# Per-head mean squares of the second block's queries and keys: column sums and turns replaced by a block-diagonal product with full-width roots

## The chip, the cores and the metric

The kernel runs on one core of a Trainium2 chip. The metric is the device time of one execution in microseconds (us), the median of several runs. Everything that follows comes from those times and from one execution recorded by the hardware profiler.

## What is computed

The program is two transformer blocks over 512 tokens of width 1024, all in float32. The change touches one step of the second block, the normalisation of its attention queries and keys:

```python
def rms_norm(x, g):
    xf = x.astype(jnp.float32)
    y = xf * lax.rsqrt(jnp.mean(xf * xf, axis=-1, keepdims=True) + RMS_EPS)
    return (y * g.astype(jnp.float32)).astype(x.dtype)

# in token_mixer of the second block
xin = h @ w_in
qa, ka, va, qm, km, vm, og, ig, fg = jnp.split(xin, cuts, axis=-1)
qa = rms_norm(qa.reshape(B, S, N_ATTN_HEADS, ATTN_HEAD_DIM), q_norm_g) * ATTN_SCALE
ka = rms_norm(ka.reshape(B, S, N_ATTN_HEADS, ATTN_HEAD_DIM), k_norm_g)
```

There are 8 heads of 64 columns, 512 tokens. So queries and keys are each 512 x 512, and each 64-long piece of a column is divided by the root of its own mean square.

## The kernel before, in words

**Layout.** Activations lie with features on the 128 partitions and the 512 tokens along the row, so a query tile `q[:, r, :]` is 128 features (two heads) by 512 tokens. Queries are four such tiles (r = 0 to 3), keys four more (r = 4 to 7). One head's mean square is a sum over 64 partitions.

**Products.** Weights come in blocks of 1 MB (`w_raw`, two buffers). ScalarE copies a block to its high part (`w_hi`, L1147), GpSimd takes the difference as the low part (`w_lo`, L489), and TensorE makes each float32 product out of three fp32r ones: high by high, high by low and low by high. An output tile of 128 x 512 is 24 matmuls (L569 to L571, or L586 to L588 for a pair, L618 to L620 for the value tiles). Everything on TensorE stands in one hand-written order; each engine runs its own list in order and they meet by semaphores.

**The order around the change.** TensorE's loop over the blocks j of the second block's input product (L995 on) has two slots per block, t = 2j and 2j + 1; each slot is one tile (t = 0 and 1, and t = 2 and 3, are pairs). Slots 0 to 3 make the queries, 4 to 7 the keys, 8 to 11 the values, slot 12 the narrow gate columns (slot 13 is empty), slots 14 on the queries and keys of the mLSTM. After slot 12 come the first attention scores (L649), which wait for all eight normalised tiles (`qk_normed` at 8).

ScalarE has the same loop (from L1508): after a tile it copies it out of its bank (L1534), squares it into one of two buffers `g[:, r % 2]` (L1535), and frees the bank. Before that it waits for the sums of the tile two before (`qn_ss`). In odd slots it also splits a weight block (L1147). VectorE's loop (from L2262) starts only behind eight products that scale `x` by the final gain (L2232, L2233).

**The norms before.** `qk_sums(r)` (L951, its matmuls L958): for each of the four groups of 128 tokens, the squares stand as the stationary operand and two columns of 1 and 0 move past them, which gives a 128 x 2 piece of sums with tokens on partitions, in bank 6. It stands after slot 3 (r = 0 and 1), slot 4 (2 and 3) and slots 5 to 8 (4 to 7). `qk_columns(e)` (L2236 on): for four tiles at once VectorE takes the mean (L2239), ScalarE the root of 128 x 32 values (L1539), VectorE inverts and refines it once (reciprocal L1732 and four small operations), and spreads it to four tiles of 128 x 512 (L2244). `qk_turn(r)` (L962, transposes L968) turns these back to features on partitions, two tiles each after slots 5, 6, 9 and 10. `qk_norm(r)` (L2251) is one VectorE operation per tile.

```python
for r in {3: (0, 1), 4: (2, 3)}.get(t + u, (t + u - 1,) if 5 <= t + u <= 8 else ()):
    qk_sums(r)
```

Of the kernel before, what the change touches and what calls it, by code (L numbers as in the profile page):

```python
# [13 lines left out]
P = 128  # L14
# [133 lines left out]
def two_blocks(nc, weights, ada, c_rows, consts, rope, tri_bias, mult_bias, tri_mask, layer_params, params, x_in, selectors, out):  # L148
    with ExitStack() as ctx:
# [49 lines left out]
        b_hi = sb("b_hi", [P, KT, S], F32R, two)  # L199
        b_lo = sb("b_lo", [P, KT, S], F32R, two)  # L200
        two.close()
        one.enter_context(nc.sbuf_tensor("region_1", [P, 2 * KT * S], F32))
        ctx.enter_context(one)

# [30 lines left out]
        next_gain = sb("next_gain", [P, KT])  # L235
        shift_parts = sb("shift_parts", [P, KT, 2], F32R)
        shift_sum = sb("shift_sum", [P, 2])

        ps = [ctx.enter_context(nc.psum_tensor(f"ps{b}", [P, S], F32)) for b in range(8)]

# [79 lines left out]
        gate_split = sem("gate_split")  # L320
        gate_scaled = sem("gate_scaled")
        qn_sq = sem("qn_sq")
        qn_ss = sem("qn_ss")
        qn_ms = sem("qn_ms")
        qn_root = sem("qn_root")
        qn_spread = sem("qn_spread")
        qn_turned = sem("qn_turned")
        qk_normed = sem("qk_normed")
        v2_ready = sem("v2_ready")
        mc_first = sem("mc_first")  # L330
# [219 lines left out]
        def _(pe):  # L550
# [397 lines left out]
                            last.then_inc(tile_done, 1)  # L948
                shift_rows(s, 1)

            def qk_sums(r):  # L951

                pe.wait_ge(qn_sq, r + 1)
                if r == AT:
                    pe.wait_ge(qn_ms, 1)
                c = 8 * (r % AT)
                for tt in range(TT):
                    last = nc.tensor.matmul(ps[6][:, c + 2 * tt:c + 2 * tt + 2], g[:, r % 2, tt * P:(tt + 1) * P],  # L958
                                            half[:, 0:P:HD], start=True, stop=True)
                last.then_inc(qn_ss, 1)  # L960

            def qk_turn(r):  # L962

                pe.wait_ge(qn_spread, r + 1)
                if r >= 2:
                    pe.wait_ge(qk_normed, r - 1)
                for tt in range(TT):
                    last = nc.tensor.transpose(ps[4 + r % 2][:, tt * P:(tt + 1) * P],  # L968
                                               g[:, 2 + r % AT, tt * P:(tt + 1) * P], ident)
                last.then_inc(qn_turned, 1)  # L970

            def a_turns():

# [21 lines left out]
            for j in range(C_OUT):  # L995
                s, t = j % 2, 2 * j
                low = low_parts(L, 4 * j)
                if j == 0:
                    plain_pair(s, low)
                    continue  # L1000
                if j == 1:
                    for u in range(2):
                        pe.wait_ge(bank_free[t + u], nth(L, LAYER_BANKS, BANK_USES[t + u]))
                    tile_pair([ps[t + u][:, :] for u in range(2)], s, (a_hi, a_lo), normed_ready(0), low)
                for u in range(2):
                    if C_VA <= j < C_IF or C_VM <= j < C_OG:
                        first = C_VA if j < C_IF else C_VM
                        token_tiles(L, 2 * first, s, (2 * u, 2 * u + 1), j - first, low, lambda n: BANK_USES[n])
                    elif j == C_IF:
                        if u == 0:  # L1010
                            tile(L, t, s, KT, 0, a_hi, a_lo, low, m=F_ROW + MH, tiles=2)
                    elif j > 1:
                        tile(L, t + u, s, KT, u * P, a_hi, a_lo, low)
                    for r in {3: (0, 1), 4: (2, 3)}.get(t + u, (t + u - 1,) if 5 <= t + u <= 8 else ()):
                        qk_sums(r)
                    for first in (AT + 1, 2 * AT + 1):
                        if t + u - first in (0, 1):
                            for e in range(2):
                                qk_turn(first - AT - 1 + 2 * (t + u - first) + e)
# [123 lines left out]
        def _(act):  # L1143
# [328 lines left out]


            L = LAYERS
            nc.scalar.activation(warm[:, :], ones[:, 0:1], ACT.Sqrt)
            nc.scalar.activation(shift_parts[:, :, 0], mod[:, 0:KT], ACT.Copy).then_inc(shift_hi, 1)
            act.wait_ge(ms_ready, nth(L, 2, 0))
# [22 lines left out]
            def silu_tanh(i):  # L1500

                act.wait_ge(mc_ready, i + 1)
                if i > 0:
                    act.wait_ge(mc_silu, i)
                nc.scalar.activation(mt[:, :], g[:, 4 + i % 2, :], ACT.Tanh, scale=0.5
                                     ).then_inc(mc_tanh, 1)

            for j in range(C_OUT):  # L1508
                for u in range(2):
                    t = 2 * j + u  # L1510
# [4 lines left out]
                    elif j in (C_VA, C_VM):  # L1515
                        if u:
                            act.wait_ge(v_halves, nth(L, 1, (C_VA, C_VM).index(j)))
                    else:
                        act.wait_ge(tile_done, nth(L, LAYER_TILES, t))
                    if j == 0:  # L1520
                        act.wait_ge(plain_scaled, t + 1)
                        nc.scalar.activation(g[:, t, :], g[:, 6 + t, :], ACT.Square, bias=shift_sum[:, t:t + 1]
                                             ).then_inc(qn_sq, 1)
                    if u and j > 0:
                        w_split(L, j + 2)
# [2 lines left out]
                            nc.scalar.activation(q[:, i, :], g[:, 6 + i, :], ACT.Identity, bias=shift_sum[:, i:i + 1])  # L1528
                        act.drain()
                    if 0 < j < C_VA:  # L1530
                        act.wait_ge(qn_ss, t - 1)
                        dst = q[:, t, :] if t < AT else k[:, t - AT, :]
                        if t >= 2:
                            nc.scalar.activation(dst, ps[b][:, :], ACT.Copy)  # L1534
                            nc.scalar.activation(g[:, t % 2, :], ps[b][:, :], ACT.Square).then_inc(qn_sq, 1)  # L1535
                            act.drain().then_inc(bank_free[b], 1)
                    if t in (AT, 2 * AT):
                        act.wait_ge(qn_ms, t // AT)
                        nc.scalar.activation(qcol[:, 1, :], qcol[:, 0, :], ACT.Sqrt).then_inc(qn_root, 1)  # L1539
# [170 lines left out]
        def _(dve):  # L1710
# [90 lines left out]
            nc.vector.memset(top[:, 1, 2:3], 0.0).then_inc(s1_split, 1)  # L1801
            nc.vector.memset(top[:, 1, 3:4], 0.0).then_inc(p1_used, 1)
            nc.vector.memset(mod[:, :], 0.0)
            dve.wait_ge(params_loaded, 16)
            for n in range(KT):
                dve.wait_ge(x_loaded[n // 2] if n > 0 else x_first, 16)
# [429 lines left out]
            def qk_columns(e):  # L2236

                dve.wait_ge(qn_ss, AT * (e + 1))
                nc.vector.tensor_scalar(qcol[:, 0, :], ps[6][:, 0:32], 1.0 / HD, EPS, ALU.mult, ALU.add).then_inc(qn_ms, 1)  # L2239
                dve.wait_ge(qn_root, e + 1)  # L2240
                refine(qcol[:, 2, :], qcol[:, 1, :], qcol[:, 0, :], qcol[:, 1, :])
                dve.drain()
                for r in range(AT):
                    nc.vector.tensor_copy(g[:, 2 + r, :].rearrange("p (t c) -> p t c", t=2 * TT),  # L2244
                                          qcol[:, 2, 8 * r:8 * r + 8].unsqueeze(2).to_broadcast([P, 2 * TT, HD])
                                          ).then_inc(qn_spread, 1)

            def qk_norm(r):
                dst, gain = (q[:, r, :], SP_QG) if r < AT else (k[:, r - AT, :], SP_KG)
                dve.wait_ge(qn_turned, r + 1)  # L2250
                nc.vector.scalar_tensor_tensor(dst, dst, sp[:, gain:gain + 1], ps[4 + r % 2][:, :], ALU.mult, ALU.mult  # L2251
                                               ).then_inc(qk_normed, 1)

            def m_gaps(h):
# [7 lines left out]
            for j in range(C_OUT):  # L2262
                for u in range(2):
                    t = 2 * j + u
                    b = t % 4
                    if t in (AT, 2 * AT):
                        qk_columns(t // AT - 1)
                    for first in (AT + 1, 2 * AT + 1):
                        if t - first in (0, 1):
                            for e in range(2):  # L2270
                                qk_norm(first - AT - 1 + 2 * (t - first) + e)
                            dve.drain()
# [272 lines left out]
def constant_matrices():  # L2545
# [4 lines left out]
            m[base + half + i, K_ROT + base + i] = -1.0  # L2550
            m[base + i, K_ROT + base + half + i] = 1.0
    for base in (0, HD):
        m[base:base + HD, K_HALF + base:K_HALF + base + HD] = 1.0
    m[:, K_ID:K_ID + P] = np.eye(P, dtype=np.float32)
    m[:, K_ONES:K_ONES + P] = 1.0
    return m
# [106 lines left out]
```

## Time and profile before

| | us |
|---|---|
| median of 3 runs | 2041.26 |
| lowest and highest run | 2041.17, 2041.50 |
| the profiled execution, first to last instruction (its span) | 2039.8 |
| TensorE busy in it | 2032.7 |
| VectorE, ScalarE, GpSimd busy | 1217.6, 897.0, 1041.2 |
| mean granted TensorE clock | 0.999 of full speed |

The time around the profiled execution's instructions has no row of its own; the span is what the profile gives, and the median of the runs is 1.5 us above it. The first row of the page says which engine is busy, the chain that ended last says on whom the end waits. Starts are microseconds from the first instruction. Matmuls overlap, so the cost of one is read from the distance between two starts, not from its own duration.

### The profile page before, as it was taken

The page shows a single profiled execution, that of the slowest core. Times are in us where ns is not written, and L with a number is a line of the kernel's source. Part 1 is how long each engine was busy: PE and PEld are TensorE (multiplying, and loading weights), DVE is VectorE, ACT ScalarE, POOL GpSimd, SP SyncE. Part 2 cuts the span into 40 slices and gives each one's busy share as a digit, 9 for nine tenths or more (in the row PEclk, how much of TensorE's full clock was granted, in tenths as well). Part 3 has the DMA queues.
Part 4 walks back from the last instruction along what each step waited for, and adds up shares of the span by engine and source line. Part 5 has one row for each costly group of instructions (what it writes and reads, how often), then busy time and mean ns, then how long its engine had stood idle before and what let it go on. Part 6 is the DMA issues. An engine that isn't in the chain of part 4 may idle for free.

```text
span 2039.8 us, 29841 instructions
## 1 busy us (share of the span) xinstructions
PE 2032.7 (100%) x10920; PEld 1715.4 (84%) x10920; DVE 1217.6 (60%) x2154; ACT 897.0 (44%) x1367; POOL 1041.2 (51%) x773
## 2 busy tenths in 40 slices
PE   9999999999999999999999999999999999999999
PEld 7788778889889877877788899898877788989898
DVE  4677336476757637854365767567445478747363
ACT  4124353536446422144445355364446544535352
POOL 5454335476565754544355755556343324556555
PEclk9999999999999999999999999999999999999999
DMA  6322212343543232221223344422221212223223
GB/s 216 99 95 93 83 62 97 121 159 111 186 145 125 104 117 95 94 96 62 83 103 133 135 157 145 165 104 104 80 102 62 83 42 95 92 104 104 104 104 104
DMA packets 36084, 222.61 MB, mean 109 GB/s; under 512 B 5308, under 2 KB 5692, under 8 KB 10336
## 3 DMA queue, kind: packets, MB, share of 16 engines
q1 hardware_dynamic: 28608, 190.66, 26.7%
q10 hardware_dynamic: 7328, 30.00, 4.3%
q8 instruction: 91, 1.49, 0.3%
q14 instruction: 57, 0.47, 0.1%
HBM read 215.65 MB, written 2.10 MB: 107 GB/s over the span
## 4 chain that ended last, share of the span: by engine, by line
PE 98%; DVE 1%; DVEq 0%; ACT 0%; DMA 0%; issue 0%; ACTq 0%
PE ps L569 18%; PE ps L571 18%; PE ps L570 18%; PE ps L733 6%; PE ps L735 6%; PE ps L734 6%; PE ps L586 4%; PE ps L587 4%; PE ps L588 4%; PE ps L649 2%; PE ps L618 1%; PE ps L620 1%; PE ps L619 1%; PE ps L670 1%; PE ps L659 1%; PE ps L703 0%
## 5 line engine op out<-in xcount | busy, mean ns | idle before, releaser
L489 POOL TENSOR_TENSOR w_lo<-w_raw,w_hi 128x512 fp32r<-128x512 f32 x544 | 734.2, 1380 | 780.8 <-ACT w_hi L1147 771.1
L1147 ACT ACTIVATE w_hi<-w_raw 128x2048 fp32r<-128x2048 f32 x134 | 256.1, 1911 | 387.8 <-PE ps L571 288.0
L569 PE MATMUL ps<-a_hi,w_hi 128*128 128x512 f32 (+1 forms) x888 | 351.8, 396 | 0.0
L571 PE MATMUL ps<-a_hi,w_lo 128*128 128x512 f32 (+1 forms) x888 | 346.2, 390 | 0.0
L570 PE MATMUL ps<-a_lo,w_hi 128*128 128x512 f32 (+1 forms) x888 | 345.8, 389 | 0.0
L503 POOL TENSOR_TENSOR w_lo<-w_raw,w_hi 128x512 fp32r<-128x512 f32 x164 | 214.7, 1331 | 160.2 <-ACT w_hi L1281 160.2
L569 PE MATMUL ps<-b_hi,w_hi 128*128 128x512 f32 x612 | 238.1, 389 | 0.0
L570 PE MATMUL ps<-b_lo,w_hi 128*128 128x512 f32 x612 | 238.1, 389 | 0.0
L571 PE MATMUL ps<-b_hi,w_lo 128*128 128x512 f32 x612 | 238.1, 389 | 0.0
L569 PEld LDWEIGHTS ps<-a_hi,w_hi 128*128 128x128 f32 (+1 forms) x888 | 165.3, 186 | 47.3 <-issue 10.8
L571 PEld LDWEIGHTS ps<-a_hi,w_lo 128*128 128x128 f32 (+1 forms) x888 | 165.3, 186 | 37.1
L570 PEld LDWEIGHTS ps<-a_lo,w_hi 128*128 128x128 f32 (+1 forms) x888 | 165.4, 186 | 34.4
L571 PEld LDWEIGHTS ps<-b_hi,w_lo 128*128 128x128 f32 x612 | 114.9, 188 | 24.0
L569 PEld LDWEIGHTS ps<-b_hi,w_hi 128*128 128x128 f32 x612 | 114.9, 188 | 23.8
L570 PEld LDWEIGHTS ps<-b_lo,w_hi 128*128 128x128 f32 x612 | 114.9, 188 | 23.7
L733 PE MATMUL ps<-a_hi,w_hi 128*128 128x256 f32 x424 | 120.2, 284 | 0.6 <-ACTq L1693 0.3
L734 PE MATMUL ps<-a_lo,w_hi 128*128 128x256 f32 x424 | 120.0, 283 | 0.0
L735 PE MATMUL ps<-a_hi,w_lo 128*128 128x256 f32 x424 | 120.0, 283 | 0.0
L1281 ACT ACTIVATE w_hi<-w_raw 128x1024 fp32r<-128x1024 f32 x82 | 85.7, 1052 | 61.1 <-DVE w_raw L1712 27.1
L1712 DVE TENSOR_TENSOR g<-ps,g 128x512 f32<-128x512 f32 (+1 forms) x116 | 73.5, 633 | 42.2 <-ACT g L1424 16.6
L1712 DVE TENSOR_TENSOR b_lo<-g,b_hi 128x512 fp32r<-128x512 f32 x86 | 63.0, 735 | 47.6 <-ACT b_hi L1410 36.2
L1825 DVE CUSTOM_DVE_ANT_0 pr<-ps,bias 128x512 f32<-128x512 f32 (+3 forms) x48 | 21.5, 486 | 114.9 <-issue 114.9
(394 smaller groups left out, 4535.0 us busy)
## 6 DMA issues: line engine op xcount, KB each, us to landing
w_raw<-in_weights SPq DMA_DIRECT2D x176, 1024.0 KB, 4.9
v<-in_ada ACTq DMA_DIRECT2D x24, 1024.0 KB, 4.9
out<-x SPq DMA_DIRECT2D x8, 256.0 KB, 2.2
x<-in_x_in SPq DMA_DIRECT2D x3, 512.0 KB, 7.0
w_raw<-in_weights SPq DMA_DIRECT2D x4, 256.0 KB, 5.7
yc<-in_c_rows ACTq DMA_DIRECT2D x2, 512.0 KB, 3.1
bias<-in_mult_bias ACTq DMA_DIRECT2D x1, 640.0 KB
x<-in_x_in SPq DMA_DIRECT2D x2, 256.0 KB, 4.9
```

Of the source, the lines that this page charges most:

```text
L489: nc.gpsimd.tensor_tensor(w_lo[:, s, piece], w_raw[:, s, piece], f32(w_hi[:, s, piece]), ALU.subtract).then_inc(w_lo_ready, 1)
L503: nc.gpsimd.tensor_tensor(quad(w_lo, s, u, kh), quad(w_raw, s, u, kh), f32(quad(w_hi, s, u, kh)), ALU.subtract).then_inc(w_lo_ready, 1)
L569: nc.tensor.matmul(o, wh, hi(kt), start=kt == 0, stop=False)
L570: nc.tensor.matmul(o, wh, lo(kt), start=False, stop=False)
L571: last = nc.tensor.matmul(o, wl, hi(kt), start=False, stop=kt == depth - 1)
L586: nc.tensor.matmul(o[u], wh, src[0][:, kt, :], start=kt == 0, stop=False)
L733: nc.tensor.matmul(o, fh[:, kt, :], mh[:, kt, :], start=kt == 0, stop=False)
L734: nc.tensor.matmul(o, fh[:, kt, :], ml[:, kt, :], start=False, stop=False)
L735: last = nc.tensor.matmul(o, fl[:, kt, :], mh[:, kt, :], start=False, stop=kt == HK - 1)
L1147: nc.scalar.activation(w_hi[:, n % 2, :], w_raw[:, n % 2, :], ACT.Copy).then_inc(w_hi_ready, 1)
L1281: return nc.scalar.activation(hi, raw, ACT.Copy)
L1712: return nc.vector.tensor_tensor(out_, a, b_, op)
```

## The change

It replaces the column sums, the narrow roots and the turns by an operation of full width for each tile.

- A 128 x 128 matrix `heads_mean` holds 1/64 in two diagonal blocks of 64 (the constant itself is changed from 1 to 1/64). ScalarE makes an fp32r copy of it once.
- ScalarE squares each tile twice: to float32 (`g[:, r % 2]`) and to fp32r (`sq_parts[..., 0, ...]`). VectorE subtracts them (`qk_low`), which gives the low part.
- TensorE (`qk_means`) makes two matmuls of 128 x 512, high and low part, into bank 4 or 5, one call after each of slots 3 to 10. From r = 2 on it waits for the norm of the tile two before.
- ScalarE (`qk_root`) takes the root of 128 x 512 means out of the bank, at the head of slots 4 to 11.
- VectorE (`qk_norm`) inverts 128 x 512 values, refines with three further operations, and multiplies.

Five semaphores go or are renamed; `qk_sums`, `qk_turn` and `qk_columns` go.

```diff
+        sq_parts = sb("sq_parts", [P, 2, 2, S], F32R, eleven)
+        heads_mean = sb("heads_mean", [P, P], F32R)
+        eps = sb("eps", [P, 1])
...
-            def qk_sums(r):
-                pe.wait_ge(qn_sq, r + 1)
-                if r == AT:
-                    pe.wait_ge(qn_ms, 1)
-                c = 8 * (r % AT)
-                for tt in range(TT):
-                    last = nc.tensor.matmul(ps[6][:, c + 2 * tt:c + 2 * tt + 2], g[:, r % 2, tt * P:(tt + 1) * P],
-                                            half[:, 0:P:HD], start=True, stop=True)
-                last.then_inc(qn_ss, 1)
-            def qk_turn(r):
-                pe.wait_ge(qn_spread, r + 1)
+            def qk_means(r):
+                pe.wait_ge(qn_split, r + 1)
                 if r >= 2:
                     pe.wait_ge(qk_normed, r - 1)
-                for tt in range(TT):
-                    last = nc.tensor.transpose(ps[4 + r % 2][:, tt * P:(tt + 1) * P],
-                                               g[:, 2 + r % AT, tt * P:(tt + 1) * P], ident)
-                last.then_inc(qn_turned, 1)
+                for e in range(2):
+                    last = nc.tensor.matmul(ps[4 + r % 2][:, :], heads_mean[:, :], sq_parts[:, r % 2, e, :],
+                                            start=e == 0, stop=e == 1)
+                last.then_inc(qn_ss, 1)
...
+                    if 3 <= t + u < 3 + 2 * AT:
+                        qk_means(t + u - 3)
...
+            nc.scalar.activation(heads_mean[:, :], half, ACT.Copy)
...
+            def qk_root(r):
+                act.wait_ge(qn_ss, r + 1)
+                if r >= 2:
+                    act.wait_ge(qk_normed, r - 1)
+                nc.scalar.activation(g[:, 2 + r % 2, :], ps[4 + r % 2][:, :], ACT.Sqrt, bias=eps[:, :]).then_inc(qn_root, 1)
...
+                    if 4 <= t < 4 + 2 * AT:
+                        qk_root(t - 4)
                     if j == 0:
                         act.wait_ge(plain_scaled, t + 1)
-                        nc.scalar.activation(g[:, t, :], g[:, 6 + t, :], ACT.Square, bias=shift_sum[:, t:t + 1]
+                        nc.scalar.activation(g[:, t, :], g[:, 6 + t, :], ACT.Square, bias=shift_sum[:, t:t + 1])
+                        nc.scalar.activation(sq_parts[:, t, 0, :], g[:, 6 + t, :], ACT.Square, bias=shift_sum[:, t:t + 1]
                                              ).then_inc(qn_sq, 1)
...
                     if 0 < j < C_VA:
-                        act.wait_ge(qn_ss, t - 1)
                         dst = q[:, t, :] if t < AT else k[:, t - AT, :]
                         if t >= 2:
                             nc.scalar.activation(dst, ps[b][:, :], ACT.Copy)
-                            nc.scalar.activation(g[:, t % 2, :], ps[b][:, :], ACT.Square).then_inc(qn_sq, 1)
+                            act.wait_ge(qn_ss, t - 1)
+                            nc.scalar.activation(g[:, t % 2, :], ps[b][:, :], ACT.Square)
+                            nc.scalar.activation(sq_parts[:, t % 2, 0, :], ps[b][:, :], ACT.Square).then_inc(qn_sq, 1)
                             act.drain().then_inc(bank_free[b], 1)
-                    if t in (AT, 2 * AT):
-                        act.wait_ge(qn_ms, t // AT)
-                        nc.scalar.activation(qcol[:, 1, :], qcol[:, 0, :], ACT.Sqrt).then_inc(qn_root, 1)
...
+            def qk_low(r):
+                dve.wait_ge(qn_sq, r + 1)
+                tt(sq_parts[:, r % 2, 1, :], g[:, r % 2, :], f32(sq_parts[:, r % 2, 0, :]), ALU.subtract
+                   ).then_inc(qn_split, 1)
+            def qk_norm(r):
+                dst, gain = (q[:, r, :], SP_QG) if r < AT else (k[:, r - AT, :], SP_KG)
+                mean_, root_, y = ps[4 + r % 2][:, :], g[:, 2 + r % 2, :], g[:, 4 + r % 2, :]
+                dve.wait_ge(qn_root, r + 1)
+                nc.vector.reciprocal(y, root_)
                 dve.drain()
+                nc.vector.scalar_tensor_tensor(root_, mean_, EPS, y, ALU.add, ALU.mult)
+                dve.drain()
+                nc.vector.scalar_tensor_tensor(root_, root_, -0.5, y, ALU.mult, ALU.mult)
+                dve.drain()
+                nc.vector.scalar_tensor_tensor(root_, root_, 1.5, y, ALU.add, ALU.mult)
+                dve.drain()
+                nc.vector.scalar_tensor_tensor(dst, dst, sp[:, gain:gain + 1], root_, ALU.mult, ALU.mult
                                                ).then_inc(qk_normed, 1)
...
-                    if t in (AT, 2 * AT):
-                        qk_columns(t // AT - 1)
-                    for first in (AT + 1, 2 * AT + 1):
-                        if t - first in (0, 1):
-                            for e in range(2):
-                                qk_norm(first - AT - 1 + 2 * (t - first) + e)
-                            dve.drain()
+                    if 4 <= t < 4 + 2 * AT:
+                        qk_norm(t - 4)
+                    if t < 2 * AT:
+                        qk_low(t)
...
-        m[base:base + HD, K_HALF + base:K_HALF + base + HD] = 1.0
+        m[base:base + HD, K_HALF + base:K_HALF + base + HD] = 1.0 / HD
```

## Rows read from the trace of the kernel before

**Rows 1.** The page: span, busy time of engines, and chain that ended last.
```profile
span 2039.8 us, 29841 instructions
PE 2032.7 (100%) x10920; PEld 1715.4 (84%) x10920; DVE 1217.6 (60%) x2154; ACT 897.0 (44%) x1367; POOL 1041.2 (51%) x773
...
PE 98%; DVE 1%; DVEq 0%; ACT 0%; DMA 0%; issue 0%; ACTq 0%
```

**Rows 2.** Timeline of PE, slots 3 to 12 (start, length, instruction, count).
```profile
1441.25 1.84 PE L958 MATMUL ps<-kc,g 128*128 128x2 f32 x16
1442.95 0.49 PE L569 MATMUL ps<-a_hi,w_hi 128*128 128x512 f32 x1
...
1448.53 1.84 PE L958 MATMUL ps<-kc,g 128*128 128x2 f32 x16
...
1455.82 0.95 PE L958 MATMUL ps<-kc,g 128*128 128x2 f32 x8
1456.63 1.07 PE L968 MATMUL ps<-kc,g 128*128 128x128 f32 x8
1457.46 0.47 PE L569 MATMUL ps<-a_hi,w_hi 128*128 128x512 f32 x1
...
1459.61 0.39 PE L569 MATMUL ps<-a_hi,w_hi 128*128 128x512 f32 x1
...
1463.01 0.95 PE L958 MATMUL ps<-kc,g 128*128 128x2 f32 x8
...
1501.18 1.13 PE L649 MATMUL ps<-k,q 64*128 64x512 f32 x4
```

**Rows 3.** Timeline of DVE, 1428 to 1500 us.
```profile
1440.49 5.34 DVE L2233 SCALAR_TENSOR_TENSOR x<-x,sp,ps 128x512 f32<-128x512 f32 x8
```

**Rows 4.** Timeline of ACT, 1428 to 1500 us.
```profile
1442.29 0.60 ACT L1534 ACTIVATE q<-ps 128x512 f32<-128x512 f32 x1 [0.84 <-PE ps L958]
1442.79 0.59 ACT L1535 ACTIVATE g<-ps 128x512 f32<-128x512 f32 x1
1443.55 1.92 ACT L1147 ACTIVATE w_hi<-w_raw 128x2048 fp32r<-128x2048 f32 x1 [0.17 <-issue]
```

**Rows 5.** Groups of DVE by form: reciprocals and a small product, 1405 to 1530 us.
```profile
L1732 DVE RECIPROCAL qcol<-qcol 128x32 f32<-128x32 f32 x2 | 0.7, 354 | 0.7 <-ACT qcol L1539 0.7
L1721 DVE RECIPROCAL ps<-qcol 128x8 f32<-128x8 f32 x1 | 0.2, 198 | 0.0
L1723 DVE SCALAR_TENSOR_TENSOR qcol<-ps,qcol 128x8 f32<-128x8 f32 x1 | 0.2, 167 | 0.1
```

**Rows 6.** Groups of DVE by form, operations 512 wide; a timeline of three with drains between.
```profile
L2390 DVE SCALAR_TENSOR_TENSOR pt<-ps,pr 128x512 f32<-128x512 f32 x2 | 1.4, 692 | 4.0 <-PE ps L1041 4.0
L2320 DVE SCALAR_TENSOR_TENSOR yc<-mt,g 128x512 f32<-128x512 f32 x3 | 2.1, 703 | 1.6 <-ACT mt L1505 1.5
L2213 DVE SCALAR_TENSOR_TENSOR a_lo<-g,mod,a_hi 128x512 fp32r<-128x512 f32 x8 | 6.0, 747 | 0.3
...
1514.20 2.40 DVE L2309 SCALAR_TENSOR_TENSOR g<-ps,sp,g 128x511 f32<-128x511 f32 x3
```

**Rows 7.** Timeline of DVE and POOL, 1395 to 1403 us: one operation beside GpSimd and alone.
```profile
1395.21 2.54 POOL L489 TENSOR_TENSOR w_lo<-w_raw,w_hi 128x512 fp32r<-128x512 f32 x2
1397.09 1.22 DVE L1777 SCALAR_TENSOR_TENSOR a_lo<-x,next_gain,a_hi 128x512 fp32r<-128x512 f32 x1 [0.21 <-issue]
...
1402.53 0.75 DVE L1777 SCALAR_TENSOR_TENSOR a_lo<-x,next_gain,a_hi 128x512 fp32r<-128x512 f32 x1 [0.22 <-issue]
```

**Rows 8.** Windows at the block's entry: busy of PE, PEld, DVE, ACT, POOL; granted clock.
```profile
1416.00:1417.00 1.00, 0.57 (x5) 0.58 (x6) 1.00 (x2) 1.00 (x1) 0.00 (x0) 1.00 0.00 0
...
1418.00:1419.00 1.00, 1.00 (x5) 1.00 (x5) 0.22 (x2) 0.75 (x3) 1.00 (x2) 0.50 0.00 0
...
1420.00:1421.00 1.00, 1.00 (x4) 0.81 (x3) 0.78 (x4) 0.00 (x0) 1.00 (x2) 0.50 0.02 8
```

**Rows 9.** Who waited for whom on PE: the one of its six groups that lies at this block's entry (total, times, longest).
```profile
PE ps L861 <- DVE yc L1790: 0.7, 1, 0.7
```

More of the change, by code:

```diff
@@ L201, in two_blocks @@
         two.close()
+        eleven = ExitStack()
+        sb("front_11", [P, (2 * AT + 3) * S], F32, eleven)
+        sq_parts = sb("sq_parts", [P, 2, 2, S], F32R, eleven)
+        eleven.close()
         one.enter_context(nc.sbuf_tensor("region_1", [P, 2 * KT * S], F32))
@@ L322, in two_blocks @@
         qn_sq = sem("qn_sq")
+        qn_split = sem("qn_split")
         qn_ss = sem("qn_ss")
-        qn_ms = sem("qn_ms")
         qn_root = sem("qn_root")
-        qn_spread = sem("qn_spread")
-        qn_turned = sem("qn_turned")
         qk_normed = sem("qk_normed")
@@ L1013, in _ @@
                         tile(L, t + u, s, KT, u * P, a_hi, a_lo, low)
-                    for r in {3: (0, 1), 4: (2, 3)}.get(t + u, (t + u - 1,) if 5 <= t + u <= 8 else ()):
-                        qk_sums(r)
-                    for first in (AT + 1, 2 * AT + 1):
-                        if t + u - first in (0, 1):
-                            for e in range(2):
-                                qk_turn(first - AT - 1 + 2 * (t + u - first) + e)
+                    if 3 <= t + u < 3 + 2 * AT:
+                        qk_means(t + u - 3)
                     pair, part = divmod(HEAD2_SLOTS.index(t + u), 4) if t + u in HEAD2_SLOTS else (-1, 0)
@@ L1803, in _ @@
             nc.vector.memset(mod[:, :], 0.0)
+            nc.vector.memset(eps[:, :], EPS)
             dve.wait_ge(params_loaded, 16)
@@ L2234, in _ @@
                                                ALU.mult, ALU.mult)
[L2236 to L2241, printed above, removed]
-                dve.drain()
[L2243 to L2246, printed above, removed]
+            def qk_low(r):
+                dve.wait_ge(qn_sq, r + 1)
+                tt(sq_parts[:, r % 2, 1, :], g[:, r % 2, :], f32(sq_parts[:, r % 2, 0, :]), ALU.subtract
+                   ).then_inc(qn_split, 1)
             def qk_norm(r):
                 dst, gain = (q[:, r, :], SP_QG) if r < AT else (k[:, r - AT, :], SP_KG)
-                dve.wait_ge(qn_turned, r + 1)
-                nc.vector.scalar_tensor_tensor(dst, dst, sp[:, gain:gain + 1], ps[4 + r % 2][:, :], ALU.mult, ALU.mult
+                mean_, root_, y = ps[4 + r % 2][:, :], g[:, 2 + r % 2, :], g[:, 4 + r % 2, :]
[7 more added lines that the diff above has]
+                nc.vector.scalar_tensor_tensor(root_, root_, 1.5, y, ALU.add, ALU.mult)
+                dve.drain()
+                nc.vector.scalar_tensor_tensor(dst, dst, sp[:, gain:gain + 1], root_, ALU.mult, ALU.mult
                                                ).then_inc(qk_normed, 1)
@@ L2265, in _ @@
                     b = t % 4
-                    if t in (AT, 2 * AT):
-                        qk_columns(t // AT - 1)
-                    for first in (AT + 1, 2 * AT + 1):
-                        if t - first in (0, 1):
-                            for e in range(2):
-                                qk_norm(first - AT - 1 + 2 * (t - first) + e)
-                            dve.drain()
+                    if 4 <= t < 4 + 2 * AT:
+                        qk_norm(t - 4)
+                    if t < 2 * AT:
+                        qk_low(t)
                     if j == C_IF:
```

## The prediction

> **What bounds the kernel now.** The page first: TensorE is busy for 2032.7 of 2039.8 us and makes 98% of the chain that ended last [rows 1]. In the waits of TensorE the longest in this part of the program is 0.7 us [rows 9]. So the end moves by what TensorE gains or loses, one for one, and the other engines are hidden as long as nothing on TensorE waits for them. The change adds waits, so the second thing to read is how far ahead of TensorE those engines are. For that I read its timeline from slot 3 to slot 12, then VectorE's and ScalarE's beside it.
>
> **TensorE's own work.** Two calls of the column sums take 1441.25 to 1442.95, 1.70 us, and again 1.70 after slot 4; a single call after slot 5 takes 1455.82 to 1456.63, 0.81, and there are four of those; two turns take 1456.63 to 1457.46, 0.83, and there are four such pairs [rows 2]. Sum: 2 x 1.70 + 4 x 0.81 + 4 x 0.83 = 9.96 us. Fifteen product matmuls take 1459.61 to 1463.01, 0.227 each, so a tile of 24 is 5.44; slot 4 takes 1442.95 to 1448.53, 5.58 [rows 2]. The 0.14 is the change-over after the float32 work; eight times 1.0 us (estimate, from that one tile). Removed: 11.0 us. Added: 16 fp32r matmuls of the width of a product, 16 x 0.227 = 3.6. Alone this would make the kernel 7.4 us faster. One 128 x 128 copy on ScalarE at the block's entry and one memset at the start are small and beside a busy TensorE: nothing.
>
> **The first wait.** The first mean product stands right behind slot 3, at 1441.25, and now needs VectorE's low part. VectorE's eight gain products run 1440.49 to 1445.83 [rows 3], and the low part stands behind them. In the old order VectorE had no part in the sums, so this cost nothing. The low part has both operands in SBUF, 0.70 us by the like row [rows 6], done 1446.5. I add 0.3 for the signal and the weight load ahead of the matmul (estimate; ScalarE's 0.17 between a drain and its next instruction is the nearest [rows 4]): TensorE resumes at 1446.8, 5.5 us late.
>
> Such a gap also costs clock. At the block's entry, after 0.7 us of waiting [rows 9] and a window in which TensorE was busy 0.57 with narrow float32 products, the granted clock stood at 0.50, the 1.2 GHz level, from 1418 to 1421 us [rows 8]. Three microseconds at half speed lose about 1.6. A gap of 5.5 is longer, so I take 1.6 once, with bounds of 0 (the drop falls inside the gap) and 3.
>
> **The chain per tile.** From r = 2 on TensorE's means of tile r wait for the norm of r - 2; ScalarE's squares of r + 2 wait for these means; the root of r - 1 stands behind these squares on ScalarE; and the norm of r - 1 waits for that root. That is a loop once per tile, whose length is set by no tile product. Its terms:
> - VectorE's norm. Four 512-wide operations: 0.69 with a PSUM operand, 0.70 and 0.70 with both in SBUF, 0.75 with a column scalar too [rows 6]. A drain adds 0.08: three operations of 0.75 take 2.40 from first start to last end with two drains between [rows 6]. With four drains: 0.69 + 0.70 + 0.70 + 0.75 + 0.32 = 3.16.
> - The reciprocal at 128 x 512 is in no row. At 8 elements it takes 198 ns, at 32 it takes 354 [rows 5]: 6.5 ns per further element, so 354 + 480 x 6.5 = 3.47 us. From below: a product of 8 takes 167 ns beside 198 [rows 5], and were a wide reciprocal no dearer than a wide product, it would take 0.7. From above, the whole 354 ns taken as proportional gives 354 x 16 = 5.7. I take 3.47, since the slope is from the same operation.
> - After the norm: signal and weight load 0.3, two mean matmuls to the end of the second 0.23 + 0.39 = 0.62, signal 0.1, two squares of 0.59 spaced by 0.50 (as L1534 and L1535 are) 1.09, drain and issue 0.17 [rows 4]. The wide root is like the 0.59 of a copy out of a bank and I give it 0.70 for the bias column. Signal 0.07. Together 3.05.
>
> One turn of the loop: 3.16 + 3.47 + 3.05 = 9.7 us. TensorE has 5.44 + 0.45 = 5.9 us of work in it, and waits 3.8. (The low part of r + 2, 0.70, fits beside the root.)
>
> By the Trainium skill (VectorE: DVE Perf Modes, Walkthrough: the 8-slice pipeline in each mode, First, the fixed hardware budget) a reciprocal is an iterative divide with a repeat count of 8; at the 0.96 GHz it gives, my estimate is 4.27 us for 512 elements and a sum 6 us higher. The two rows above give 6.5 ns per element rather than 8.3, and the sum stays with them.
>
> **VectorE beside GpSimd.** The same operation with both inputs in SBUF takes 1.22 us while GpSimd splits weights and 0.75 alone [rows 7]. In slots 5, 7 and 11 ScalarE's weight split follows directly on the root, GpSimd then works about 5 us, and the last three operations of norms 1, 3 and 7 lie under it: 3 x 0.47 = 1.4 each. For norm 4, which meets the split of slot 9 at its end, I take 0.5.
>
> **The sum, in time.**
> - Means 0 from 1446.8 to 1447.3; slot 4 with the slow clock ends 1447.3 + 5.44 + 1.6 = 1454.3.
> - Means 1 end 1454.9, squares 3 end 1456.1, root 0 ends 1457.0, norm 0 runs 1457.1 to 1463.7.
> - Norms 1 to 4, one turn of the loop each: + 4 x 9.7 + 1.4 + 1.4 + 0.5 = 1505.8.
> - No squares follow tile 7, so norms 5 and 6 run back to back: + 2 x 6.7 = 1519.2. TensorE has its last two wait-bound calls here (means 6 and 7); slot 11 ends about 1518.5.
> - Root 7 waits for slot 11 and ends 1519.4; norm 7 ends 1519.4 + 0.1 + 6.6 + 1.4 = 1527.5.
> - The scores wait for all eight norms: 1527.8 with signal and weight load. Slot 12 ends at 1524.0, so this is a wait too. In the old trace they start at 1501.18 [rows 2].
>
> Difference + 26.6. Behind the scores the order is the old one, and TensorE is again the bound. The ledger agrees: - 7.4 of work, + 5.5 + 1.6 for the first gap, about + 23 for five waits of 3.8 to 5.2 and one of 1.3 after slots 5 to 10, + 3.8 before the scores. The profiled execution would have a span of 2066.4; against the median of the runs, 1.5 us above the span of before, I forecast 2041.26 + 26.6 = **2067.9 us**.
>
> **Rivals.**
> 1. *The loop fits under the tiles, and the narrow work goes for nothing (faster).* Then only the TensorE ledger counts: 2041.26 - 7.4 = 2033.9, with the first wait gone as well. It needs a loop of at most 5.9 us. The 3.05 around the norm and the 3.16 of its four products alone are 6.2, so it decides against it even with a free reciprocal; only shorter signals or operations than in any row would bring it. Chance 0.03.
> 2. *Only the first wait binds.* The reciprocal is as cheap as a product and all else is slightly shorter: - 7.4 + 5.5 + 0 to 1.6 gives 2039.4 to 2041.0. For it speaks that the reciprocal's width is extrapolated over a factor of 16; against it the slope. Chance 0.03.
> 3. *The loop binds, but with a reciprocal well under the slope.* At 2.5 us each of the eight norms is 1.0 shorter, less what the tiles of slots 9 to 11 then set: 2061. Chance 0.1.
> 4. *A longer norm.* Were the slope beyond 32 elements a quarter steeper than between 8 and 32 (354 + 480 x 8.1 = 4.25 us), or GpSimd in the reciprocal's way too, each norm would be 0.8 longer, eight times: 2067.9 + 6.4 = 2074. For it speaks that two short operations, mostly fixed cost, carry the slope. Chance 0.16. The Trainium skill's rule above gives about this time.
> 5. *The clock falls again and again.* Each wait of 3.8 us could bring the 1.2 GHz level as in [rows 8]. In the middle that is mostly hidden, since a slow tile of at most 7.5 us still fits in 9.7; the mean matmuls in the loop would cost 0.4 more a turn, and the last wait up to 1.6 after the scores: 2067.9 + 7 x 0.4 + 1.6 = 2072.3. Chance 0.18.
>
> The forecast itself has 0.5. A measurement can tell about 0.2% (4 us) from no change. **Faster** by more than that: 0.03. **Within** it: 0.03, rival 2 and all its edges. **Slower**: 0.94. The range takes in rivals 3, 4 and 5 with the bounds of the clock and of the contention (none at all is - 5): 2057 to 2077.
>
> **What the changed profile would show.** Among the waits of TensorE a new line for the mean products, released by VectorE: one of 5 to 6 us and five or six of 3 to 4.5. A reciprocal of 128 x 512, eight of them, at 3.4 to 3.5 us: the term on which most hangs, 8 us of the sum per 1 us. Mean products about 9.7 us apart from the third on. Scores starting near 1528. A window at 0.50 clock in slot 4. I am wrong if TensorE shows no waits there, or if the eight reciprocals take under 1 us.

## The result and the profile after

| | before | after |
|---|---|---|
| median of the runs shown with the result (5 each), us | 2041.26 | 2071.80 |
| ratio, with its 95% interval | | 1.015 [1.0140, 1.0161] |
| span of the profiled execution, us | 2039.8 | 2071.4 |
| mean granted TensorE clock | 0.999 | 0.992 |

The kernel is 1.5% slower, 30.5 us; 26.6 were forecast (2067.9, with a range of 2057 to 2077). Where did the time go? The page of the changed kernel, to be read against [rows 1]:

```profile
span 2071.4 us, 29735 instructions
PE 2039.0 (98%) x10840; PEld 1715.5 (83%) x10840; DVE 1269.2 (61%) x2175; ACT 906.1 (44%) x1382; POOL 1042.5 (50%) x773
...
PE 93%; DVE 4%; DVEq 1%; ACT 1%; issue 0%; DMA 0%; ACTq 0%; POOL 0%
```

TensorE's share of the chain that ended last falls from 98 to 93%, and VectorE has 4 in place of 1. VectorE's busy time grows by 51.6 us. That it is 61% busy over the whole program tells nothing here: 50.4 of the 51.6 us lie in a stretch of 91 (1440 to 1531, where the same work before took 61). The profiled execution is the slowest of the five (2073.21 us). TensorE is idle 32.4 us (span less busy) where it was idle 7.1, and its own busy time is not less but 6.3 more, although it has 80 instructions fewer. Both need a closer look. First, for whom it waits (total, times, longest), which answers to [rows 9]:

```profile
PE ps L961 <- DVE q L2254: 13.2, 4, 5.0
PE ps L961 <- DVE sq_parts L1710: 5.1, 1, 5.1
PE ps L653 <- DVE k L2254: 3.6, 1, 3.6
PE ps L961 <- DVE k L2254: 3.5, 2, 1.8
```

L961 are the mean products, L2254 the last operation of a norm, L653 the first scores. The sum is 25.4 us: one wait for the first low part (5.1), four and two for norms of the two tiles before (13.2 and 3.5), one before the scores (3.6). The mean products in TensorE's timeline, and the scores, which answer to the last of [rows 2]:

```profile
1446.44 1.22 PE L961 MATMUL ps<-sq_parts,heads_mean 128*128 128x512 f32 x2 [5.08 <-DVE sq_parts L1710]
1453.90 0.62 PE L961 MATMUL ps<-sq_parts,heads_mean 128*128 128x512 f32 x2
1463.20 1.19 PE L961 MATMUL ps<-sq_parts,heads_mean 128*128 128x512 f32 x2 [3.20 <-DVE q L2254]
1474.82 1.19 PE L961 MATMUL ps<-sq_parts,heads_mean 128*128 128x512 f32 x2 [3.86 <-DVE q L2254]
1484.68 0.71 PE L961 MATMUL ps<-sq_parts,heads_mean 128*128 128x512 f32 x2 [1.17 <-DVE q L2254]
1495.82 1.19 PE L961 MATMUL ps<-sq_parts,heads_mean 128*128 128x512 f32 x2 [4.95 <-DVE q L2254]
1505.94 0.71 PE L961 MATMUL ps<-sq_parts,heads_mean 128*128 128x512 f32 x2 [1.66 <-DVE k L2254]
1513.91 0.78 PE L961 MATMUL ps<-sq_parts,heads_mean 128*128 128x512 f32 x2 [1.81 <-DVE k L2254]
...
1530.79 1.44 PE L653 MATMUL ps<-k,q 64*128 64x512 f32 x4 [3.64 <-DVE k L2254]
```

From 1463.20 to 1505.94 they stand 11.6, 9.9, 11.1 and 10.1 us apart, where a tile with its mean product is 5.9 us of work. Where a pair takes 1.19 us and not 0.62, the clock is down. What fills such a turn is in VectorE's timeline, here norm 1 and the beginning of the next turn:

```profile
1465.54 0.69 DVE L1710 TENSOR_TENSOR sq_parts<-g,sq_parts 128x512 fp32r<-128x512 f32 x1 [2.49 <-ACT sq_parts L1536]
1466.39 3.35 DVE L2246 RECIPROCAL g<-g 128x512 f32<-128x512 f32 x1 [0.16 <-ACT g L1503]
1469.82 0.69 DVE L2248 SCALAR_TENSOR_TENSOR g<-ps,g 128x512 f32<-128x512 f32 x1
1470.59 0.75 DVE L2250 SCALAR_TENSOR_TENSOR g<-g 128x512 f32<-128x512 f32 x1
1471.41 1.59 DVE L2252 SCALAR_TENSOR_TENSOR g<-g 128x512 f32<-128x512 f32 x1
1473.09 1.58 DVE L2254 SCALAR_TENSOR_TENSOR q<-q,sp,g 128x512 f32<-128x512 f32 x1
1477.17 0.69 DVE L1710 TENSOR_TENSOR sq_parts<-g,sq_parts 128x512 fp32r<-128x512 f32 x1 [2.49 <-ACT sq_parts L1536]
```

The reciprocal is 3.35 us. The idle 2.49 before each of these low parts is the way through TensorE and ScalarE. The last two operations of norm 1 take 1.6 us where they take 0.69 and 0.75 in norm 0. GpSimd splits weights from 1468.24 to 1474.12. The operation from 1470.59 lies in that stretch too, with both operands in SBUF, and takes 0.75; why it is spared is not shown. And the windows (busy of PE, PEld, DVE, ACT, POOL, then the granted clock), which answer to [rows 8]:

```profile
1442.00:1444.00 2.00, 0.00 (x0) 0.00 (x0) 2.00 (x4) 0.99 (x2) 0.97 (x1) 1.00 0.05 8
...
1446.00:1448.00 2.00, 1.56 (x4) 1.28 (x5) 0.98 (x2) 0.30 (x1) 0.00 (x0) 0.53 0.55 234
1448.00:1450.00 2.00, 2.00 (x7) 1.58 (x6) 0.69 (x1) 1.83 (x3) 0.00 (x0) 0.61 0.00 0
...
1475.00:1480.00 5.00, 5.00 (x12) 3.92 (x13) 2.65 (x2) 2.26 (x4) 0.00 (x0) 0.50 0.60 210
...
1495.00:1500.00 5.00, 4.18 (x10) 3.34 (x11) 2.06 (x3) 1.77 (x3) 0.12 (x1) 0.50 0.63 211
...
1515.00:1520.00 5.00, 5.00 (x18) 3.97 (x17) 4.69 (x5) 0.00 (x0) 0.00 (x0) 0.72 0.34 141
...
1530.00:1535.00 5.00, 4.21 (x11) 2.56 (x12) 3.48 (x8) 1.80 (x2) 0.18 (x1) 0.66 0.61 210
```

TensorE stands at the 1.2 GHz level (0.50), for some microseconds each time, after the first wait, after those of 3.20, 3.86 and 4.95 us, after the last before a mean product (1.81), and after the one before the scores. After the waits of 1.17 and 1.66 us the granted clock is 1.00. This is why its busy time grew: between 1475 and 1480 it was busy throughout and began 12 matmuls, where 22 fit at full clock. How much busy time that is in all, e4 below tells: it has the same 10840 matmuls and no wait in this stretch, and TensorE is busy 2026.5 us in it, 12.5 less than here.

### The profile page after: what moved, and what is told of

It is laid out like the page before. It is cut to its first block, busy times and chain, and to the rows that moved or that the text cites. A ratio compares the mean times of both kernels' runs of the same rounds, so it can differ in the third digit from the quotient of the medians.

```text
span 2071.4 us, 29735 instructions
## 1 busy us (share of the span) xinstructions
PE 2039.0 (98%) x10840; PEld 1715.5 (83%) x10840; DVE 1269.2 (61%) x2175; ACT 906.1 (44%) x1382; POOL 1042.5 (50%) x773
## 4 chain that ended last, share of the span: by engine, by line
PE 93%; DVE 4%; DVEq 1%; ACT 1%; issue 0%; DMA 0%; ACTq 0%; POOL 0%
PE ps L573 18%; PE ps L575 17%; PE ps L574 17%; PE ps L737 6%; PE ps L739 6%; PE ps L738 6%; PE ps L590 3%; PE ps L591 3%; PE ps L592 3%; PE ps L653 2%; PE ps L674 1%; PE ps L663 1%; PE ps L622 1%; PE ps L623 1%; PE ps L624 1%; DVE g L2246 1%
```

## The experiments

All times are medians. The kernel before, run beside them, had 2040.19 us in the first group (e1 to e4), 2041.22 in the second (e7, e10, e9) and 2040.62 in the third (e11, e12). Ratios are to it, with their 95% intervals. The changed kernel stood beside a kernel before of 2041.26 us, so a difference of medians between it and a run of the first group can be 1.1 us too large. The figure in square brackets behind a difference between groups is therefore that of the two distances from the kernel before. Line numbers of an experiment are its own.

### e1_gain_later: the first wait taken away

```diff
                     if t < 2 * AT:
                         qk_low(t)
+                    if t == 1:
+                        for n in range(KT):
+                            final_gain(n)
```
(in place of the same loop ahead of the slots; the means go to `ps[6 + r % 2]`)

> The eight gain products of VectorE move behind the low parts of tiles 0 and 1, and the means go to banks 6 and 7, so that bank 4 stays the gain's. Theory (the first wait and its slow clock shift the whole chain, one for one): no wait of 5 us before the first mean product, norm 0 starts near 1450 instead of 1456.5, and the time falls by 6 to 7 us, to about 2065. Rival (the first wait is absorbed by the later ones, which would grow): the scores start at the same time and the time falls by 1 us or less.

Measured: 2064.11 us, ratio 1.0116 [1.0099, 1.0133], 7.7 us [6.6] below the changed kernel. The row of 5.1 us for the low part is gone from TensorE's waits, and most of the others is left (18.4 us of 20.3):

```profile
PE ps L961 <- DVE q L2254: 12.5, 4, 4.3
PE ps L653 <- DVE k L2254: 3.6, 1, 3.6
PE ps L961 <- DVE k L2254: 2.3, 1, 2.3
```

The scores start at 1521.08, 9.7 us earlier (slot 3 itself ends 1.8 us earlier in this execution, so 7.9 are the change's), and norm 0 begins at 1449.21. So the first wait shifts the chain with all that comes behind it; the later waits do not absorb it.

### e2_copy_for_reciprocal: the norm made shorter

```diff
-                nc.vector.reciprocal(y, root_)
+                nc.vector.tensor_copy(y, root_)
```

> A copy of the same shape stands in place of the reciprocal; the inversion is left out. Theory (the loop's length is the norm's, 3.35 us of it the reciprocal): each norm is 2.9 us shorter, seven or eight of them lie on the chain, and the time falls by 20 to 23 us, to about 2050, with mean products 6.7 us apart in place of 9.6. Rival (the waits come from the handshake between the engines, not from the norm's length): the mean products stay over 8.5 us apart and the time falls by 5 us or less.

Measured: 2050.13 us, ratio 1.0045 [1.0030, 1.0059], 21.7 us [20.6] below the changed kernel. The copy takes 0.43 us. The mean products of tiles 2 to 5 start at 1460.00, 1468.21, 1474.67 and 1482.91, 7.6 us apart on average rather than 6.7, since every second turn has GpSimd in it:

```profile
PE ps L961 <- DVE sq_parts L1710: 5.1, 1, 5.1
PE ps L961 <- DVE q L2254: 4.7, 4, 2.1
PE ps L653 <- DVE k L2254: 0.8, 1, 0.8
```

The waits for norms fall from 20.3 us (13.2 + 3.6 + 3.5) to 5.9 (4.7 + 0.8 and one of 0.4 not shown). The norm's length sets the waits, and the reciprocal is about two thirds of what the change costs.

### e3_four_banks: the handshake loosened

```diff
-                if r >= 2:
-                    pe.wait_ge(qk_normed, r - 1)
+                if r >= 4:
+                    pe.wait_ge(qk_normed, r - 3)
...
-                    last = nc.tensor.matmul(ps[4 + r % 2][:, :], heads_mean[:, :], ...
+                    last = nc.tensor.matmul(ps[4 + r % 4][:, :], heads_mean[:, :], ...
```

> The means take banks 4 to 7 in turn, so TensorE waits for the norm of four tiles before and no more of two before. Theory (with two banks the loop through all engines sets the pace; with four only VectorE's own sum does, about 7.4 us a tile with the low part and GpSimd's share): TensorE waits no more in slots 5 to 9 but some 13 to 15 us before the scores, and the time falls by 12 to 16 us, to about 2058. Rival (VectorE's sum of work was the bound already): the same waits move to the scores and the time stays within 3 us of 2072.

Measured: 2063.23 us, ratio 1.0110 [1.0093, 1.0127], 8.6 us [7.5] below the changed kernel, against 12 to 16 expected. That lies between the theory's 12 to 16 and the rival's 3 at most; the pattern of the waits is the theory's:

```profile
PE ps L653 <- DVE k L2254: 15.2, 1, 15.2
PE ps L961 <- DVE sq_parts L1710: 5.1, 1, 5.1
PE ps L573 <- ACT v L1547: 2.9, 1, 2.9
```

TensorE waits for no norm until the scores and there for 15.2 us. VectorE works from 1455.86 to 1519.66 without a gap that counts: 63.8 us for eight norms and five low parts. One norm there, with both neighbours:

```profile
1493.00 1.08 DVE L2250 SCALAR_TENSOR_TENSOR g<-g 128x512 f32<-128x512 f32 x1
1494.15 1.62 DVE L2252 SCALAR_TENSOR_TENSOR g<-g 128x512 f32<-128x512 f32 x1
1495.86 1.58 DVE L2254 SCALAR_TENSOR_TENSOR k<-k,sp,g 128x512 f32<-128x512 f32 x1
1497.37 3.34 DVE L2246 RECIPROCAL g<-g 128x512 f32<-128x512 f32 x1
```

That is 8.0 us a tile, against 5.9 of TensorE. So loosening the loop through three engines removes the smaller part of the loss; VectorE's sum of work keeps the larger. Three things in the trace go against the expected gain: operations beside GpSimd at 1.6 us (1.2 had been put in), value tiles that ScalarE now frees later, since roots that wait for norms stand ahead of them (2.9 us), and the clock after the long wait, which e10 takes up. How they share it was not separated.

### e4_no_norm_gain_later: TensorE's ledger alone

As e1, with the reciprocal and the three refining lines of `qk_norm` left out.

> As e1_gain_later, and the reciprocal and the three refining products are left out, so that a norm is one product (the output is then multiplied by the root). Theory (TensorE alone is the bound once nothing waits, and its work is 7.4 us less than before): about 2034 us, no wait over 1 us in slots 3 to 12. Rival (the means or the extra ScalarE work cost something of their own): 2037 us or more, or a wait that is left.

Measured: 2034.76 us, ratio 0.9966 [0.9952, 0.9980], that is 6.9 us below before by the ratio and 5.4 by the medians. No wait of TensorE between slots 3 and 12 is left, the mean products stand 5.94 us apart, and the scores start at 1494.30, where before has 1501.18: 6.9 us again, with slot 3 ending at the same time within 0.1 us. The TensorE side of the change is worth about 7 us. Two mean matmuls take 5.94 - 5.44 = 0.50 us there, where the forecast had 0.45.

### e7_four_banks_gain_later

e1 and e3 together (banks 6, 7, 5, 4 in turn), and the roots of tiles 4 to 7 ahead of ScalarE's waits for the value tiles.

> Both mends of waits together: four banks (6, 7, 5, 4 in turn) and the gain products behind the first two low parts; ScalarE also takes roots 4 to 7 ahead of its waits for the value tiles. Theory (with four banks VectorE's list of work sets the end, and it now begins about 6.5 us earlier): about 2057 us, one wait of 14 to 17 us before the scores and no other over 1 us. Rival (with four banks the start does not matter, since TensorE only waits at the end): 2062 us or more.

Measured: 2055.97 us, ratio 1.0069 [1.0054, 1.0085]. One wait of 14.8 us before the scores as expected, 0.5 for the last low part (at 1484.62), and one of 3.6 for a value tile, which the expectation had ruled out. The mends together give 15.8 us [15.8], half of the loss. The other half is VectorE's list of work, as e11 shows, where only that list is shorter.

### e10_filled_wait: what the clock takes

```diff
+                            pe.wait_ge(bank_free[2], nth(L, LAYER_BANKS, BANK_USES[14]))
+                            for _ in range(48):
+                                nc.tensor.matmul(ps[2][:, :], wcols(w_hi, s, KT, 0, 0, P), a_hi[:, 0, :], start=True, stop=True)
                             pe.wait_ge(qk_normed, 2 * AT)
```

> As e3_four_banks, with 48 matmuls of 128 x 512 that compute nothing of use put into the 15 us wait before the scores. Theory (the wait costs twice: itself, and then 5 us in which the granted clock stands at 0.5, some 2.5 us): with TensorE kept busy the clock stays at 1.00 after the scores and the time falls by 2 to 3 us below e3_four_banks, to about 2060.5. Rival (the clock plays no part in the result): the same time as e3_four_banks within 1 us, or more if the filling overlaps the scores.

Measured: 2060.26 us, ratio 1.0091 [1.0076, 1.0106]. That is 3.0 us [4.0] below e3, against 2 to 3 expected. The intervals of e3 and e10 overlap, so the times alone do not settle it. The traces do. First the windows of e3, then those of e10:

```profile
1510.00:1515.00 5.00, 0.00 (x0) 0.00 (x0) 4.92 (x3) 0.00 (x0) 2.34 (x2) 0.50 0.31 82
...
1520.00:1525.00 5.00, 5.00 (x12) 2.82 (x12) 2.40 (x7) 2.23 (x4) 0.00 (x0) 0.51 0.00 0
```
```profile
1510.00:1515.00 5.00, 5.00 (x24) 4.14 (x23) 4.84 (x4) 0.00 (x0) 3.13 (x2) 1.00 0.17 33
...
1520.00:1525.00 5.00, 4.48 (x19) 3.16 (x20) 3.20 (x8) 2.38 (x4) 0.00 (x0) 1.00 0.01 3
```

After the empty wait TensorE begins 12 matmuls in 5 us, after the filled one 19. The stretch from the first score to the end of the span, in which nothing was changed, measures it best (span less the start of the scores, one execution each):

| kernel | wait before the scores | scores to the end, us |
|---|---|---|
| before | none | 2039.8 - 1501.2 = 538.6 |
| e11_no_refining | none | 2031.7 - 1492.7 = 539.0 |
| e10, filled | 1.7 | 2059.6 - 1520.5 = 539.1 |
| e1 | 3.6 | 2061.4 - 1521.1 = 540.3 |
| after | 3.6 | 2071.4 - 1530.8 = 540.6 |
| e7 | 14.8 | 2055.9 - 1515.0 = 540.9 |
| e3 | 15.2 | 2061.2 - 1519.7 = 541.5 |

Against 538.6 before, a wait ahead of the scores costs 1.7 to 2.0 us more than itself when it is 3.6 us long and 2.3 to 2.9 when it is 15, and work put into it takes all but 0.5 of that back.

### e9_rows and e12_rows_sum_later: few roots, cheap sums

For four tiles at once the mean squares are gathered as 8 rows of 512 in one bank, inverted and refined once, split, and spread:

```diff
+                for e in range(2):
+                    last = nc.tensor.matmul(ps[7 - r // AT][0:8, :], heads_mean[:, 6 - 2 * i:14 - 2 * i], sq_parts[:, r % 2, e, :],
+                                            start=i == 0 and e == 0, stop=i == AT - 1 and e == 1)
...
+                for e in range(2):
+                    last = nc.tensor.matmul(ps[5 - r % 2][:, :], spread[0:8, i * P:(i + 1) * P], y_parts[0:8, e, :],
+                                            start=e == 0, stop=e == 1)
```

> The idea of the change with the roots kept few: for four tiles at once, fp32r products with an 8-column matrix gather the heads' mean squares as 8 rows of 512; one root, one reciprocal and one refinement of 8 x 512 serve four tiles; their high and low parts are spread to 128 partitions by two fp32r matmuls per tile; the gain products stand partly behind tile 3. Theory (the wide reciprocal per tile is what failed, while the fp32r products are cheaper than the column sums and turns): TensorE has 32 x 0.227 = 7.3 us in place of 11.0, no wait over 1 us, and the time is 3 to 4 us below before, about 2037 us. Rival (the two reciprocals of 3.35 us in a row with high and low parts still come too late for slot 7 or 10): a wait of 2 us or more there and no gain.

Measured: 2040.99 us, ratio 0.9997 [0.9988, 1.0006]: no difference, where 3 to 4 us had been expected. It had one wait, of 1.1 us, for the low part of tile 1, and its slots from 3 to the scores take 59.5 us (1441.66 to 1501.11), 0.5 less than before. The 32 matmuls cost more than 0.227 each:

```profile
1468.12 1.21 PE L982 MATMUL ps<-y_parts,spread 8*128 8x512 f32 x4
1469.25 0.51 PE L633 MATMUL ps<-w_hi,a_hi 128*128 128x512 f32 x1
1469.59 0.40 PE L634 MATMUL ps<-w_lo,a_hi 128*128 128x512 f32 x1
```

Four spreading matmuls take 1.13 to the next start rather than 0.91, and the first product behind them 0.34 rather than 0.23. There are four such rows: about 1.3 us. With the wait of 1.1 that is 2.4 of the 3.2 us that are missing between the 3.7 of the ledger and the 0.5 measured; the rest has no row that names it. In e12 the sum of tile 1 goes one slot later (`{3: (0,), 4: (1, 2), ...}`).

> As e9_rows, with the sums of tile 1 one slot later, since TensorE waited 1.1 us for its low part after slot 3. Theory (that wait is on the path, one for one): the wait is gone and the time about 1 us below e9_rows, 2039.9 us or so, against before a difference of 0.5 to 1.5 us that the runs may not tell from none. Rival (ScalarE's squares of tile 3, which now wait a slot longer, come late for the next): a new wait of 1 us or more and no gain.

Measured: 2039.83 us, ratio 0.9995 [0.9986, 1.0004]. The wait is gone from the list and the stretch from slot 3 to the scores takes 58.2 us, 1.2 less than in e9, but against before the runs show no difference. A form with few roots is safe and gains too little to be seen.

### e11_no_refining: the version that beats both

e7, with the norm cut to two operations. The step of refinement after root and reciprocal is left out, so the inverse root is no more exact than ScalarE's root. What that costs in precision no run here measures, so this kernel is not quite the same computation as the other two.

```diff
                 nc.vector.reciprocal(y, root_)
                 dve.drain()
-                nc.vector.scalar_tensor_tensor(root_, mean_, EPS, y, ALU.add, ALU.mult)
-                ...
-                nc.vector.scalar_tensor_tensor(dst, dst, sp[:, gain:gain + 1], root_, ALU.mult, ALU.mult
+                nc.vector.scalar_tensor_tensor(dst, dst, sp[:, gain:gain + 1], y, ALU.mult, ALU.mult
```

> As e7_four_banks_gain_later, but the norm is only the reciprocal of ScalarE's root and one product; the three refining operations are left out. Theory (VectorE's list per tile falls from 7.2 us and GpSimd's share to 4.9 and a smaller share, below the 5.9 us that TensorE has per slot, so that nothing waits and only TensorE's ledger of - 7 is left): 2034 to 2036 us, no wait over 1 us between slots 3 and 12, and clearly faster than before. Rival (some hand-over of the norms is still late at the end, since norm 7 stands behind all others): a wait of 2 us or more before the scores and 2037 us or more.

Measured: 2033.63 us, ratio 0.9966 [0.9953, 0.9978]: 7.0 us faster than before and 38 us faster than the changed kernel. VectorE at a tile with GpSimd beside it, and the last norm:

```profile
1454.15 3.35 DVE L2248 RECIPROCAL g<-g 128x512 f32<-128x512 f32 x1
1457.58 1.51 DVE L2250 SCALAR_TENSOR_TENSOR q<-q,sp,g 128x512 f32<-128x512 f32 x1
1459.23 1.57 DVE L1712 TENSOR_TENSOR sq_parts<-g,sq_parts 128x512 fp32r<-128x512 f32 x1
...
1489.22 0.75 DVE L2250 SCALAR_TENSOR_TENSOR k<-k,sp,g 128x512 f32<-128x512 f32 x1
```

At its worst a tile is 6.6 us of VectorE (1454.15 to 1460.72); at its best 4.9 (from 1449.29), which is 5.7 on average against TensorE's 5.9 per slot. The last norm ends at 1489.97, 2.7 us ahead of the scores at 1492.68. Those start 8.5 us earlier than before; 1.7 of that is slot 3, which ends at 1439.55 in this execution (1441.25 before), so 6.8 are the change's. The full TensorE ledger of e4 is there, with the norm in it. Whether the two banks and the old place of the gain products would also do with this short norm was not tried.

## Why the prediction was right, and what it missed

**What bounds it, and the direction.** The mechanism is the forecast's: TensorE waits where it was said to, for whom it was said, and a loop once per tile sets the pace. Rivals 1 and 2 fall by the waits alone. The sizes of the waits were not as forecast. Five of 3.8 to 5.2 us and one of 1.3 had been put between the mean products, about 23 us; they were 3.2, 3.9, 1.2, 5.0, 1.7 and 1.8, together 16.7. The turns are as long as forecast all the same, because TensorE does part of its work at half clock where it would have waited. That is rival 5's mechanism, inside the main case.

**TensorE's ledger.** Forecast - 7.4 us; e4, where nothing waits, shows - 6.9, mostly because a pair of mean matmuls takes 0.50 and not 0.45.

**The first wait.** Forecast 5.5 us, measured 5.1. Its slow clock was put at 1.6; mean products 0 and 1 stand 7.5 us apart where 5.94 is a turn at full clock, so it was 1.5. Norm 0 was to begin at 1457.1 and began at 1456.5. By e1 both together are worth 6.6 to 7.7 us.

**The reciprocal.** Forecast 3.47 us from 6.5 ns per element, measured 3.35, eight times. The rule of the Trainium skill (VectorE: DVE Perf Modes, Walkthrough: the 8-slice pipeline in each mode, First, the fixed hardware budget), from whose repeat count of 8 an estimate of 4.27 us followed, is not borne out as a price: the measurement is 22% below it. Rival 4 in that form falls, and rival 3 too.

**The loop.** Forecast 9.7 us, and 1.4 more in every second turn; measured 9.9 and 10.1 (even) and 11.6 and 11.1 (odd). That norm 4 ended at 1505.8, as forecast, is luck as well as reason. Norm 0 ended 0.6 us early (1463.05 for 1463.7). The split of slot 9, for which norm 4 had been given 0.5, fell under norm 5. Each norm without a split beside it took 6.5 us rather than 6.6. Against that stood the dearer neighbour in norms 1 and 3 and, at half clock, longer mean matmuls in the loop, the 0.4 a turn that the forecast had left to rival 5.

**Where the missing 4 us are.** By the medians 3.9 us are missing (2071.8 against 2067.9). The profiled execution, the slowest of the five, has a span of 2071.4 where 2066.4 was forecast, 5.0 us more: 3.0 ahead of the scores (1530.8 against 1527.8) and 2.0 behind their start. Three terms were mis-sized.
- *GpSimd beside VectorE.* The step took 0.47 us for each operation from [rows 7] (1.22 against 0.75). Under the four-part weight split they take up to 1.6, so 0.9 more. In norm 1 that is 1.8 us in place of 1.4. In norm 5, for which nothing was put in, it is 1.6:

```profile
1509.90 1.33 DVE L2250 SCALAR_TENSOR_TENSOR g<-g 128x512 f32<-128x512 f32 x1
1511.31 1.62 DVE L2252 SCALAR_TENSOR_TENSOR g<-g 128x512 f32<-128x512 f32 x1
```

  So mean product 7, which waits for norm 5, starts at 1513.9, where the forecast's terms give 1512.8.
- *The clock in slot 11.* The slot was to end about 1518.5. It starts 1.1 us late by norm 5, and its first eight matmuls stand 0.43 us apart in place of 0.227, which makes 1.6 more. ScalarE's root 7 waits for it and begins at 1521.7, where 1518.7 was forecast: 3.0 us late. VectorE stands idle 2.3 us ahead of the last norm, and the scores, at 1530.8, are late by the same 3.0.
- *The clock after the last wait.* It had been left to rival 5 as a possibility, at up to 1.6. The table under e10 shows 2.0.

Rival 5, the clock that falls again and again, is thus in the trace: its price in the loop is mostly hidden, as was said, since a slow tile fits into a turn; in slot 11 and at the end, 1.6 and 2.0 us, it is not. Its own figure, 2072.3, is the nearest of all to the measured 2071.8, but only in part for its reason: it had 2.8 us in the loop and 1.6 behind the scores.

**What stays open.** No run moves GpSimd's split away from a norm, so the price of that neighbour is read from operations that coincide in the traces, and why some of them are spared is not known. Why the clock fell after the wait of 1.81 us and not after that of 1.66 was not looked for either.

## What to carry to other kernels

An operation that takes work off a full engine is worth its ledger only if its partners keep up: add up each partner's time per turn, with the neighbours that slow it, and compare that with the bound engine's time per turn. Here TensorE had 5.9 us of work a tile. A hand-over through two banks made a turn of 9.9 to 11.6 us out of it, and a late first low part came on top: 7 us of gain became 30 of loss. With both mended (e7) the kernel was still 15 us slower than before, since VectorE alone needs about 8.0 us a tile (as read in e3); with 5.7 us (e11) the whole gain was there. Moving a result from narrow (tokens on partitions, 32 columns) to wide (512 columns) makes every later operation dearer, the reciprocal above all (0.35 to 3.35 us). And what stands in the queue ahead of a new hand-over (here the eight gain products, 6.6 us with the clock behind them) costs as much as a slow operation in it.

## What was not expected of the hardware

- The reciprocal did not get cheaper with fewer partitions: 8 x 512 took 3.34 us in e9_rows, and 128 x 512 took 3.35.
- A product with two SBUF operands takes up to 1.8 us beside GpSimd's weight split (1.78 for a low part in e7), more than twice its 0.69, but not every one does (0.75 at 1470.59 in the changed kernel); a reciprocal, with one such operand, is not slowed: that from 1476.69 in e11 lies beside a split that begins at 1477.46 and takes 3.34.
- Idle stretches of 3.6 us before the scores cost 1.7 and 2.0 us of clock, one of 15.2 us cost 2.9, and 48 matmuls of no use took it back to 0.5.
- The spreading matmuls of e9, with 8 rows of stationary operand, took 0.28 us each in rows of four, not 0.227; what of that is the short operand and what the change of bank was not tried.
